# Two layers of a hybrid model in one kernel: the six places of the split weights get other start offsets

## What is computed

```python
def first_block(x, ...):                      # D_MODEL 1024, SEQ 256
    mix = _hybrid_mixer(_rmsnorm(h), ...)     # h @ w_in (1024 x 11280), two branches, w_out
    h = h + mix
    ffn = _hierarchical_moe(_rmsnorm(h), ...) # 32 experts, hidden 512, 2 chosen of each token
    ...
def _conv_ffn(h, w_up, conv_w, conv_b, w_down):
    u = h @ w_up                              # 1024 x 5632
    ...                                       # convolution over 3 tokens, silu(gate) * up
    return (...) @ w_down                     # 2816 x 1024
```

## Time and profile before

| | |
|---|---|
| time of three runs | 1516.57, 1518.22 (median), 1519.96 us |
| profiled execution | 1512.32 us, span 1511.0 us |
| granted clock of PE, mean | 0.967 |
| PE busy | 1377.9 us (91%) |
| DVE busy | 865.1 us (57%) |
| ACT busy | 680.5 us (45%) |
| idle of PE that an expert's transfer ended (the two longest entries) | 44.1 and 24.6 us |

### The profile page before, as it was taken

The page is one execution under the profiler, slowest core; times in us unless marked ns, Lnnn a source line. Parts: engine busy times, 40 slices in busy tenths (PEclk is TensorE's granted clock), DMA queues, the critical chain, the costliest instruction groups (busy, mean ns, idle before and its releaser), DMA issues.

```text
span 1511.0 us, 27444 instructions
## 1 busy us (share of the span) xinstructions
PE 1377.9 (91%) x11609; PEld 1178.5 (78%) x11609; DVE 865.1 (57%) x1558; ACT 680.5 (45%) x1185; POOL 13.2 (1%) x14
## 2 busy tenths in 40 slices
PE   7999999999989877877777689999999999999999
PEld 7999999999966434443333389999999987799998
DVE  6786463575522211121121278978898769788886
ACT  6544554644442111111111267566555558666554
POOL 1000000000000000000000010000000000000000
PEclk9999999999989888899999999999999999999999
DMA  7454354568899999999999854335565532546552
GB/s 240 143 174 159 122 170 138 183 237 326 319 400 426 426 426 423 426 426 427 425 426 427 330 168 141 112 113 175 187 203 190 165 114 77 195 141 223 186 177 84
DMA packets 171089, 372.04 MB, mean 246 GB/s; under 512 B 6976, under 2 KB 137280, under 8 KB 146384
## 3 DMA queue, kind: packets, MB, share of 16 engines
q1 hardware_dynamic: 170960, 370.21, 65.8%
HBM read 369.14 MB, written 1.05 MB: 245 GB/s over the span
## 4 chain that ended last, share of the span: by engine, by line
PE 56%; DMA 23%; DVE 11%; ACT 6%; issue 2%; SPq 1%; DVEq 0%; ACTq 0%
PE bank L612 14%; PE bank L613 14%; PE bank L614 14%; DMA wu<-in_expert_w_down_dram 13%; DMA wu<-in_expert_w_up_dram 7%; DVE part L576 3%; PE bank L1740 3%; PE bank L1712 2%; ACT part L565 2%; PE bank L1778 2%; PE bank L843 1%; DMA raw<-in_w_in_dram 1%; DVE lo L576 1%; PE bank L1792 1%; DVE t L915 1%
## 5 line engine op out<-in xcount | busy, mean ns | idle before, releaser
L576 DVE TENSOR_TENSOR part<-raw,part 128x1024 fp32r<-128x1024 f32 x251 | 300.1, 1216 | 152.0 <-ACT part L565 151.3
L612 PE MATMUL bank<-XH,part 128*128 128x256 f32 x1176 | 334.1, 284 | 4.8 <-DVE part L576 1.5
L613 PE MATMUL bank<-XL,part 128*128 128x256 f32 x1176 | 328.3, 279 | 0.0
L614 PE MATMUL bank<-XH,part 128*128 128x256 f32 x1176 | 328.2, 279 | 0.0
L565 ACT ACTIVATE part<-raw 128x1024 fp32r<-128x1024 f32 x251 | 256.0, 1051 | 84.1 <-PE bank L614 45.1
L612 PEld LDWEIGHTS bank<-XH,part 128*128 128x128 f32 x1176 | 222.6, 189 | 8.0 <-issue 4.7
L613 PEld LDWEIGHTS bank<-XL,part 128*128 128x128 f32 x1176 | 221.7, 189 | 1.1
L614 PEld LDWEIGHTS bank<-XH,part 128*128 128x128 f32 x1176 | 222.0, 189 | 0.0
L1740 PE MATMUL bank<-wu,xg 128*32 128x256 f32 x2048 | 171.0, 437 | 49.4 <-DMA wu<-in_expert_w_up_dram 44.1
L1740 PEld LDWEIGHTS bank<-wu,xg 128*32 128x32 f32 x2048 | 72.7, 122 | 122.8 <-DMA wu<-in_expert_w_up_dram 60.6
L1778 PE MATMUL bank<-wu,hidT 128*32 128x256 f32 x1024 | 75.5, 412 | 34.7 <-DMA wu<-in_expert_w_down_dram 24.6
(11 more groups left out here) (413 smaller groups left out, 2758.4 us busy)
## 6 DMA issues: line engine op xcount, KB each, us to landing
wu<-in_expert_w_gate_dram SPq DMA_DIRECT2D x64, 1024.0 KB, 26.3
wu<-in_expert_w_up_dram SPq DMA_DIRECT2D x64, 1024.0 KB, 26.7
wu<-in_expert_w_down_dram SPq DMA_DIRECT2D x64, 1024.0 KB, 26.7
raw<-in_w_in_dram SPq DMA_DIRECT2D x44, 1024.0 KB, 5.0
raw<-in_ffn_w_up_dram SPq DMA_DIRECT2D x44, 1024.0 KB, 4.9
raw<-in_ffn_w_down_dram SPq DMA_DIRECT2D x22, 1024.0 KB, 5.0
raw<-in_hgrn_w_in_dram SPq DMA_DIRECT2D x16, 1024.0 KB, 5.3
raw<-in_w_branch_ret_dram SPq DMA_DIRECT2D x8, 1024.0 KB, 6.7
```

Of the source, the lines that this page charges most:

```text
L576: dve.tensor_tensor(lo_of(u), v, hi_of(u), ALU.subtract).then_inc(*WL.inc(u))
L612: pe.matmul(dst, first[0], first[1], start=start, stop=False)
L613: pe.matmul(dst, second[0], second[1], start=False, stop=False)
L614: return pe.matmul(dst, third[0], third[1], start=False, stop=stop)
```

## The change

Two places now make a pair of 8448 bytes (33 x 256). The first begins at 0, the second at 4160 (64 past a multiple of 256); the pairs take the same room as before, so nothing else moves. Each unit takes its offset from a table with an entry for each place: `STAND` where it stands still, `MOVE` where it moves narrow, and 0 or 48 values where it moves wide. The order of the instructions of all engines, their waits and the DMAs are the same as before; only addresses differ.

```diff
-PAD = 32
-PART = 4 * (1024 + PAD)
-APART = 16
+PAIR = 8192 + 256
+STAND = (15, 30, 13, 27, 1, 15)
+MOVE = (15, 18, 14, 14, 8, 2)
...
     for made_ in (hi, lo):
         for _ in range(2):
-            made_ += [at(fixed.skip(PART), [P, 1024 + PAD], F32R, "part") for _ in range(2)]
+            pair = fixed.skip(PAIR)
+            made_ += [at(pair, [P, 1040], F32R, "part"), at(pair + 4160, [P, 1072], F32R, "part")]
...
-    end2 = (top - 4 * PART) // 256 * 256
-    for i in range(2):
-        hi.append(at(end2 + 2 * PART * i, [P, 1024 + PAD], F32R, "hi"))
-        lo.append(at(end2 + 2 * PART * i + PART, [P, 1024 + PAD], F32R, "lo"))
+    end2 = (top - 2 * PAIR) // 256 * 256
+    for i, made_ in enumerate((hi, lo)):
+        pair = end2 + PAIR * i
+        made_ += [at(pair, [P, 1040], F32R, "part"), at(pair + 4160, [P, 1072], F32R, "part")]
...
-            units.append((len(tiles) - 1, v, 0 if cut is halves_k and y > 256 else APART))
+            units.append((len(tiles) - 1, v, STAND if cut is not halves_k else MOVE if y <= 256 else (0, 48) * 3))
...
-        o = units[u][2]
+        o = units[u][2][slot_of(u)]
```

More of the change, by code:

```diff
@@ L420, in layout @@
     where += [us_at + 8192 * i for i in (5, 6, 7)] + [gla_at, gla_at + 8192] + [us_at + 8192 * i for i in (0, 1)]
-    where += [raw_at + 8192, raw_at] + [split_at + 2 * PART * i for i in (1, 3, 0, 2)] + [xh_at]
+    where += [raw_at + 8192, raw_at] + [split_at + PAIR * i for i in (1, 3, 0, 2)] + [xh_at]
     W_RAW, W_HI, W_LO = (16, 15), (19, 17), (20, 18)
```

## The result

Over 20 runs each the changed kernel took 1523.05 us (1520.12 to 1528.39) and the kernel before 1517.39 us (1512.17 to 1523.02). The ratio is 1.0042, with a 95% interval of 1.003 to 1.0054: slower, where the forecast was faster by 0.5% with a range that ended at 1520.5 us. The profiled execution of the changed kernel has a span of 1523.7 us. Its page (busy time; then the splits and their mean durations) answers to the earlier trace rows.

What follows compares the result with a forecast made beforehand. Outside the experts, the prediction took the distances between PE's call starts as the bound. Gains of 2.5 + 2.2 + 1.5 + 1.0 = 7.2 us, taken from 1518.22, gave 1511.0 us, range 1502.5 to 1520.5.

Steps and rivals of the forecast that it cites:

- What bounds the kernel: Outside the experts: number of PE's calls times the distance between their starts; 16.9 us lie above the best distances.
- Two states: PE's 256-column calls: two lasting distances, 117.9 ns (long) and 113.3 (short); a place only makes entering or leaving one likely.
- Wide units: Both networks and MLA: all begin on a multiple of 256, twelve calls fall to about 2.72 us; gain 2.5 us.
- Other units that stand still: Standing units besides steps' first tiles: states found much as before; gain 1.0 us, bounds 5.0 gain and 12.0 loss.
- The first tile of a step: Networks, behind wide units in 20 steps: takes its state over from them; gain 2.2 us, between 0 and 4.4.
- Narrow units: Narrow units that move, 1205 undisturbed calls at unseen phases: gain 1.5 us, bounds 4.5 gain and 1.0 loss.
- ACT and DVE at odd words: Operands of standing units on odd 4-byte words: DVE priced at 0, ACT at most 0.10 us a unit, taken as 0.
- The rival that came true: Long state catches more, up to 320 us and in steps' second tiles: at most 10.5 us slower, likely 1523 us; chance 0.12.
- Passing to the end: Whole kernel: nearly all of the 7.2 us should reach the end, because PE is full where it lies.

Runs made afterwards that it cites:

- the map: PE alone, output not computed: a split unit's products with weights at 64 phases (starts modulo 256 bytes, 4-byte steps), without pause and behind other calls; 113.3 ns at 64.
- the seven entries: PE alone, output not computed: standing units at each phase, entered behind two float32 calls and two calls of 64 to 190 columns; at 76 all seven short.
- wide_only: Kernel before with only wide units changed, to begin on a multiple of 256 bytes at every place; ratio 0.999 (0.9973 to 1.0008).
- stand_76: Kernel before with standing units at phase 76 at every place, and equal phases for both halves at places 4 and 5; ratio 0.9937 (0.9918 to 0.9956).
- stand_only: Kernel before with the changed kernel's phases for units that stand still; at places 4 and 5 moving units adjusted to fit; ratio 1.0045 (1.0029 to 1.006).
- the 39 entries tested: PE alone, output not computed: seven coarse entries at each phase, and 32 in steps of 4 columns at ten phases; at 76 28 of 32 end short.
- best_76: Kernel before with phases from the map at all places: standing units 76, narrow 28 or 192, wide 0; ratio 0.9942 (0.992 to 0.9964).
- best_52: As best_76, with 52 in place of 76 for the units that stand still; ratio to the kernel before 1.0035 (1.0016 to 1.0055).
- stand_108: Kernel before with standing units at phase 108 everywhere, and equal phases for both halves at places 4 and 5; ratio 1.0123 (1.0093 to 1.0153).

## Why the prediction was wrong

- **What bounds the kernel** was right: outside the experts, PE's start-to-start distances, not waits or the other engines. So was the disagreement with the Trainium skill's one distance ("TensorE: Matmul & The Clock Gate", section "Wait — 56ns, not 53.3ns?"): no unit with 256 columns in any of these runs settles at the 109.2 ns that its formula gives. Each call here has a weight load of its own (11609 of each on the page); whether that accounts for the 4.1 ns between 109.2 and the best 113.3 was not tested.
- **Two states** was the premise that failed first. The prediction took it that there are two lasting distances at every phase and that "a place only makes it likely to enter or leave one". In the map a phase has distances of its own: 113.3, 115.5, 116.7, 117.8, 118.3, 120, 122 and more. At 39 of 64 phases every entry ends at the same one, and at 57 none of the seven entries ends at 113.3.
- **Wide units**: 2.5 us forecast, 2.5 us measured (3.2 to 0.7), in the changed kernel and in wide_only. It was the one term with a row at the new phase. By the time alone it can't be seen (wide_only).
- **Other units that stand still**: this step failed. The text priced phases by how near they are in bytes ("New phases at places 0 to 3 are 4, 8, 12 and 20 bytes from the old ones, so I expect the states to be found much as before") and took a gain of 1.0. The map shows that being near in bytes says nothing: 60 and 64 lie 6 ns apart. With the first tiles of the steps these units cost 13.0 us more, where a gain of 3.2 was forecast; by the shares, 0.57 short became 0.21. The bound of 12.0 us for all turning long was also too low, since "long" isn't 117.9 everywhere: 119 to 120 is common in the changed kernel, and the map has 122 and 133.
- **The first tile of a step**: the 2.2 us rested on a state handed over by the wide units. wide_only refutes it: 2.83 us a unit as before. stand_76 shows the reverse, with wide units in the first network at their old phases and the tile behind them short, 2.72 us a unit: at 64 and at 76 the tile's own phase decides. At 52 the wide units do play a part. In the first network the first unit behind them begins at 52 and takes 2.76 us in stand_only, with wide units at their old phases, and 2.88 us in the changed kernel, with wide units at 0: short wide units made it longer there. In the second network this unit, at 60, takes 2.87 us in both. There are also 18 such steps and not 20, nine in each network, so the bound was 4.0 us and not 4.4.
- **Narrow units**: a gain of 1.5 forecast, 2.6 more measured. The new phases 136, 120, 56 and 72 are all at 120 ns in the map. The loss is outside the prediction's bound of 1.0, which took 117.8 ns as the longest distance. That none of the new phases had been seen before was said, and a value between the bounds was no estimate.
- **ACT and DVE at odd words**: priced at 0, measured 1051 and 1217 ns a unit against 1051 and 1216. The rule in the Trainium skill, "Vector Engine (DVE) Microarchitecture Reference", section "Measured stream behaviour on trn2", on pairs that start on an odd word does not carry over to one contiguous run of 1024 words, as DVE's subtraction has it here with one source and the result on an odd word.
- **The rival that came true** is the second, given 0.12 and 1523 us, with 1523.05 measured. Its condition, over 560 and for a measurable loss 1200 more long calls, was met with 1887. Its mechanism was half right: the long states do catch more, but at place 0 it isn't a matter of a pause; at phase 60 none of the 39 entries tested ends short. That its 1523 us was met is luck: it bounded the loss in distances at 10.5 us, 13.1 came, and fewer than half of them reached the medians.
- **Passing to the end**: "nearly all" was too much for the whole. In the networks all of it passes. From the first call of the first network to the first call behind it, the distances of best_76, stand_76, wide_only, the changed kernel, best_52 and stand_108 differ from before by -2.5, -1.8, -0.7, 3.0, 3.2 and 7.4 us, and the time by -2.3, -1.8, -0.6, 3.1, 3.4 and 7.4; in the second network they agree within 0.2 us too. In the HGRN layer it doesn't show: 1.7 us less of distances in best_76 went with 1.0 us more of time. In the first block single profiles can't tell: wide_only, with nothing changed there, ends the experts' stretch 4.0 us later than before. An estimate comes from the medians: behind this stretch the changed kernel took 5.1 us more in its profile, and the whole 5.7 us more, which leaves about 1 us for the 7.4 us of distances that the first block lost. In stand_108 the same subtraction leaves about 5 of 9.6. So part of the first block's loss was probably absorbed; where is not shown.

Open: what in the chip makes the two operands' starts matter, and why a state holds. The runs show the dependence on the difference of the starts and on the entry, not its cause. Not tested either is a high and a low half at different phases, as places 4 and 5 had them before, where 0.9 of the calls were short.

## What to carry over

Where PE is full, read the distance between the starts of its calls by unit, not its busy share; if one shape has two distances, the operands' start addresses may be worth trying (here 9 of 1517 us). Don't choose phases by nearness or by one trial: map the distance over all phases with PE alone, enter each phase in many ways, and take the one that is short from nearly every entry (here the stationary operand 76 bytes past the moving one, modulo 256: 28 of 32 entries). A phase that is short once, like 52 or 64, may lose in the model, as best_52 did.

## What wasn't expected of the hardware

A shift of one 4-byte word in an operand's start moved `fp32r` calls of 256 columns between 113.3 and 119.7 ns; the slowest phases, 28 to 36, held 133.3 ns when entered without a pause and 117 to 120 behind another call. The pattern depends on the difference of the two operands' starts: moving the activation by 64 bytes moved the map without a pause by 64 at 61 of 64 phases. Calls of 512 columns had 226.6 to 240 ns, depending on the phase.
